# Row work of the experts in the attention turns: two units at every second turn of a head in place of one at each

## The reference, cut to what matters

```python
def peer(h):                                  # 1024 tokens, 8 heads, 16 experts of each
    q = h @ w_pq                              # scores against 2 x 128 keys, top 16 of each half,
    experts, gates = top16(sums(top16(q . keys1), top16(q . keys2)))   # best 16 of the sums
    a = gelu(einsum('td,thkd->thk', h, u_experts[experts])) * softmax(gates)
    return einsum('thk,thkd->td', a, v_experts[experts])
```

## Time and profile before

| | before |
|---|---|
| median of 3 runs | 3424.23 us |
| the profiled execution, its own time | 3428.18 us |
| its span, first to last instruction | 3426.4 us |
| TensorE busy | 2763.8 us (81%) |
| VectorE busy | 2176.9 us (64%) |
| ScalarE busy | 1371.4 us (40%) |
| GpSimd busy | 1224.1 us (36%) |
| gathers of expert rows | 1024, 1073.81 MB, 76.3% of 16 engines' span |
| mean DMA rate over the span | 364 GB/s |
| DMA busy share, slices 7 to 40 of 40 | 0.9 or more in nearly all |
| attention turns of groups 1, 2, 3 | about 665 to 790, 1412 to 1556, 2194 to 2334 us |

### The profile page before, as it was taken

One profiled execution on the slowest core, in us unless ns is written; L12 is line 12 of the kernel. 1 busy time (PEld: TensorE's weight loads), 2 busy tenths in 40 slices (PEclk: granted clock), 3 DMA queues, 4 the chain that ended last, 5 costly groups with the idle time before them and its releaser, 6 DMA issues.

```text
span 3426.4 us, 29234 instructions
## 1 busy us (share of the span) xinstructions
PE 2763.8 (81%) x8208; PEld 1489.1 (43%) x8208; DVE 2176.9 (64%) x4668; ACT 1371.4 (40%) x3703; POOL 1224.1 (36%) x1051
## 2 busy tenths in 40 slices
PE   7988878788887789788888689798887866666666
PEld 7665455354334355454335355364334322222222
DVE  1121156876774778766775767766675787777766
ACT  1112123493533343573533332583533333333333
POOL 0000013443443344334443333334343444544553
PEclk9997989999998999899998899899998889889988
DMA  6322359999999999989999999989999999999998
GB/s 239 135 99 92 129 221 382 418 382 418 427 413 386 401 425 426 375 319 376 422 427 404 385 402 397 368 334 376 420 415 402 424 426 427 427 426 415 426 427 351
DMA packets 187458, 1247.42 MB, mean 364 GB/s; under 512 B 22048, under 2 KB 31264, under 8 KB 41376
## 3 DMA queue, kind: packets, MB, share of 16 engines
q0 software_dynamic: 147456, 1073.81, 76.3%
q1 hardware_dynamic: 36384, 154.98, 11.6%
q10 hardware_dynamic: 3456, 16.78, 1.2%
HBM read 1224.77 MB, written 20.71 MB: 364 GB/s over the span
## 4 chain that ended last, share of the span: by engine, by line
PE 42%; DMA 33%; DVE 9%; ACT 6%; issue 4%; POOL 3%; DVEq 2%; ACTq 1%; POOLq 0%; SPq 0%
DMA rows<-in_experts,idx 28%; PE ps L906 17%; PE ps L939 10%; PE ps L925 6%; POOL rows L608 3%; DMA wbuf<-in_w_conv 3%; DVE rows L1291 2%; DVE acc_v L1302 2%; PE ps L957 2%; PE ps L890 1%; ACT L767 1%; DMA wbuf<-in_w_pq 1%; PE ps L1091 1%; PE ps L970 1%; PE ps L975 1%
## 5 line engine op out<-in xcount | busy, mean ns | idle before, releaser
L608 POOL DMA_INDIRECT rows<-in_experts,idx x1024 | 1220.4, 1192 | 2178.0 <-PE ps L906 1175.8
L906 PE MATMUL ps<-rows,diag 128*128 128x512 f32 x3072 | 1584.8, 656 | 355.5 <-ACT diag L664 321.4
L1291 DVE CUSTOM_DVE_ANT_0 rows<-rows,hn 128x1024 f32<-128x1024 f32 x1024 | 1236.7, 1223 | 682.0 <-DMA rows<-in_experts,idx 666.0
L906 PEld LDWEIGHTS ps<-rows,diag 128*128 128x128 f32 x3072 | 616.2, 209 | 1165.1 <-issue 591.2
L653 ACT ACTIVATE gelu<-dots 128x1 f32<-128x1 f32 x1024 | 206.6, 202 | 1383.8 <-DVE dots L1291 1369.9
L939 PE MATMUL ps<-T,wbuf 128*128 128x256 f32 x1600 | 399.7, 403 | 95.0 <-DMA wbuf<-in_w_conv 47.8
L939 PEld LDWEIGHTS ps<-T,wbuf 128*128 128x128 f32 x1600 | 320.2, 202 | 197.0 <-DMA wbuf<-in_w_conv 53.5
L925 PE MATMUL ps<-wbuf,T 128*128 128x512 f32 x768 | 362.1, 610 | 18.8 <-ACT T L815 7.5
L664 ACT ACTIVATE diag<-ident,weight 128x128 f32<-128x128 f32 x768 | 308.5, 402 | 75.3 <-PE ps L906 11.9
L657 ACT ACTIVATE weight<-gelu,gate 128x1 f32<-128x1 f32 x1024 | 301.7, 295 | 74.8 <-DVE gate L1270 2.9
L1302 DVE SCALAR_TENSOR_TENSOR acc_v<-rows,weight,acc_v 128x1024 f32<-128x1024 f32 x256 | 327.7, 1280 | 1.6 <-ACT weight L657 1.6
(11 more groups left out here) (200 smaller groups left out, 1824.3 us busy)
## 6 DMA issues: line engine op xcount, KB each, us to landing
wbuf<-in_w_conv SPq DMA_DIRECT2D x24, 1024.0 KB, 10.0
wbuf<-in_w_o SPq DMA_DIRECT2D x16, 1024.0 KB, 9.0
wbuf<-cross_a SPq DMA_DIRECT2D x16, 1024.0 KB, 9.3
wbuf<-cross_b SPq DMA_DIRECT2D x16, 1024.0 KB, 9.1
wbuf<-in_w_pq SPq DMA_DIRECT2D x16, 1024.0 KB, 9.4
rows<-in_experts,idx POOLq DMA_INDIRECT x1024, 12.3
wbuf<-in_w_cq SPq DMA_DIRECT2D x8, 768.0 KB, 8.5
wbuf<-in_w_ckvr SPq DMA_DIRECT2D x8, 576.0 KB, 6.8
```

The lines of the kernel that those rows point to most:

```text
L608: pool.indirect_dma_start(out=rows[n % RR][:], out_offset=None, in_=w["experts"][:, :], in_offset=bass.IndirectOffsetOnAxis(ap=idx[:, b % ...
L906: mm = pe.matmul(ps[:, 6 + half, :], diag[:, m % DIAGS, :], rows[n % RR][:, D + half * HALFC:D + (half + 1) * HALFC], start=(k == 0), stop ...
L1291: dve.tensor_tensor_reduce(out=rows[n % RR][:, 0:D], in0=rows[n % RR][:, 0:D], in1=hn[:, b % 3, :], scale=1.0, scalar=0.0, op0=ALU.mult, o ...
```

## The change

In the three loops over turns of a head, an engine takes two units at every even turn, and none at the odd ones. There are 20 turns, so 10 times 2 units where there were 20 times 1. Nothing else is changed.

```diff
 (ScalarE)
                 for i in range(HH + 5):
-                    if i < HH + 4:
-                        take(work, ROOM["head"])
+                    if i < HH + 4 and i % 2 == 0:
+                        take(work, 2 * ROOM["head"])
 (TensorE)
                     if 3 <= i < HH + 3:
                         turn_probs(i - 3, 0)
-                    take(work, ROOM["head"])
+                    if i % 2 == 0:
+                        take(work, 2 * ROOM["head"])
                     if i >= 4:
                         weigh(i - 4)
 (VectorE)
                 for i in range(HH + 4):
-                    take(work, ROOM["head"])
+                    if i % 2 == 0:
+                        take(work, 2 * ROOM["head"])
                     if i < HH:
                         biggest(i)
```

## The result

The changed kernel takes 3442.36 us (median of 8 runs), the kernel before 3421.1 us in its 8 runs: a ratio of 1.0056, with a 95% interval of 1.0034 to 1.0078. It is slower, by about 19 us by the ratio and by 21 us between the medians, just outside the 17 us within which the prediction saw no change that can be told. A second comparison gave 1.0059 [1.0042, 1.0077]. The profiled execution took 3448.18 us with a span of 3446.3, 19.9 us more than before.

What follows compares the result with a forecast made beforehand. Transfers were taken to bound the kernel nearly everywhere; 7.3 - 2 - 3 + 12.3 - 2 gave +12.6 us, so 3437 us (+0.37%), no change that can be told, leaning slower, with a range of 3418 to 3456.

Steps and rivals of the forecast that it cites:

- The bound: Whole kernel: transfers bound it nearly everywhere; attention group 1 close to that limit, group 2 not, group 3 nearly TensorE-bound.
- What it saves: ScalarE in the attention stages: about 14 table loads fewer per group, 18 us each, 54 us over three groups.
- The ring: Attention rounds: VectorE's units, ScalarE's tail, exp, score, maximum wait in a loop; 12.04, 13.75, 14.0 us; chance 0.72.
- piece: VectorE, within the ring: one piece of the choice of experts per round, taken at 1.8 us, ends 1.0 and 2.3.
- the copy's 0.95: Six rounds of each group: one copy of outputs, 0.95 us, added to the sum of the rounds.
- entry: Start of each attention stage: item 3's score waits behind one more unit, 4.1 us, in three groups +12.3 us.
- exit: Behind item 15: one unit fewer is left; group 1 gives back 0 to 4.7 us, taken at -2, elsewhere nothing.
- the clock rival: TensorE in groups 1 and 3: longer waits halve its clock as in group 2; +30 us, 3454; chance 0.12.
- The sum: Three attention stages: rounds +7.3, -2, -3, entry +12.3, exit -2, in all +12.6 us.
- The ends of the range: The forecast's own range: -6 us below and about +28 above, so 3418 to 3452.
- The table loads': Rival, attention stages: table loads were the limit and the ring isn't; -38 us, 3386; chance 0.10.
- nothing moves: Rival, attention stages: transfers, TensorE and an equal ring in group 2 still set the pace; 3424; chance 0.06.

Runs made afterwards that it cites:

- without table loads: The kernel before with Copy in place of gelu, so no table load stands in the turns: ratio 0.9909 [0.9878, 0.9940].
- second profile: The changed kernel run once more with nothing altered, for a second profile: ratio 1.0059 [1.0042, 1.0077] against the kernel before.
- second pair: Changed kernel and kernel before, each run once more unaltered and profiled again: ratios 1.0059 and 0.9971 against the kernel before.
- 8 buffers: The changed kernel with 8 buffers for the diagonal matrices in place of 4: ratio 1.0040 [1.0014, 1.0066] against the kernel before.
- the ring broken: The changed kernel with VectorE taking its two units one turn earlier than ScalarE and TensorE: 3403.48 us, ratio 0.9939 against the kernel before.

## Why the prediction was right, and where its sizes were off

**The bound.** That group 2 and not group 1 had room, group 3 being near TensorE's limit, held: without table loads the stages fell by 5.4, 28.6 and 7.3 us.

**What it saves.** 14 loads a group were counted, 40 went in all, 13.3 a group.

**The ring.** Its terms stand in the trace one by one. In the round shown the piece took 2.3 us to the next product where 1.8 was taken as the mean, and the score's way to its maximum 1.39 us where 1.29 was: 12.04 + 0.5 + 0.1 is the 12.66 measured. The sum can be made for each round of group 1, with that round's own piece in place of 1.8 and the copy's 0.95 in the fifth:

| round of group 1 | piece | sum | measured | TensorE at half clock |
|---|---|---|---|---|
| 1 | 1.0 | 11.2 | 11.4 | 0 |
| 2 | 2.3 | 12.5 | 12.7 | 0 |
| 3 | 2.0 | 12.2 | 12.3 | 0 |
| 4 | 1.1 | 11.4 | 12.8 | 6.8 |
| 5 | 2.3 | 13.5 | 13.7 | 0 |
| 6 | 1.7 | 12.0 | 12.8 | 6.8 |

Every round at full clock is met within 0.2 us, and the two with a half-clock stretch are 1.4 and 0.8 over. In the second profile the stretches lie in rounds 3 and 5, and these are the ones that are 0.5 and 0.6 over; the others are 0.1 to 0.3 over. So most of the 0.4 us by which the mean round (12.6) lies above the sum with its copy (12.2) is the clock, and little is the ring.

**The stages were right in part by luck.** What each part was to change, and what it changed in the two pairs of profiles (us; rounds, entry to item 3's score, exit behind item 15's):

| | summed | first pair | second pair |
|---|---|---|---|
| group 1 | +7.3, +4.1, -2 | +9.7, +1.5, -1.6 | +6.4, +2.5, -0.5 |
| group 2 | -2, +4.1, 0 | +0.7, +5.9, -2.6 | -4.1, +5.4, -4.7 |
| group 3 | -3, +4.1, 0 | +2.0, +3.2, +3.8 | +2.1, +3.1, +3.8 |

Group 1's stage was to be +9.4 and was +9.6, then +8.4, but in the first pair its rounds were 2.4 us over and its entry 2.6 under. The exit of group 2 gave back 2.6 and 4.7 us where nothing was taken. The kernel before is no fixed mark either: its six rounds of group 1 took 65.9 and 68.2 us.

**Group 3 is the term of the sum that was mis-sized.** It was taken at -3 for the rounds, +4.1 for the entry and 0 for the exit, +1.1 in all, and came to +8.9 and +9.0. Five of its rounds took 14.3 us against 14.0. The rest lies where TensorE was at half clock: one round of 17.9 us, and 3.8 us more in the exit, where the prediction had nothing since VectorE isn't last there. So the clock rival was partly right: in group 3 above all, and by about 2 us in the rounds of group 1. Group 3's stage with 8 buffers, where the half-clock stretches are fewer, is 7.9 us shorter. By the clock records inside its group 3 stage the changed kernel was at the lower level for 31.5 us (31.6 in its second profile), the kernel before for 14.6 (14.8), the one with 8 buffers for 11.8. Why it stayed low so much longer with 4 buffers than with 8 was not settled. The sign given for this rival, a clock under about 0.9 in group 1, could not decide: it was 0.88 there before the change and 0.87 after.

**The entry.** From the last copy of keys to item 3's score the stages took 26.9, 26.4 and 28.1 us and take 28.4, 32.3 and 31.2: +10.5 where +12.3 was summed, and +11.0 in the second pair. The total is near, but the forecast had it as 4.1 us in each group, and it was 1.5, 5.9 and 3.1.

**The sum.** +12.6 was forecast, +19 measured by the ratio. In the profiles the three stages gained 22.6 us, 10 more than summed: 7.8 of them in group 3, 2.0 in group 2 and 0.2 in group 1. The rest of the kernel took 2.7 us less, so the span gained 19.9. The ends of the range don't follow from their terms: the low end's add up to -3.4 us, not -6 (7.3 - 7 - 3 + 4 - 4.7), and the high end's to +27. The measured time lies inside either way.

**The rivals.** The table loads' was right in what it said of the kernel before and wrong in that no other ring would take over. That nothing moves doesn't fit: two comparisons gave 1.0056 and 1.0059, twice the 0.3% by which an identical program differed from itself, and groups 1 and 3 were longer in both pairs of profiles. Of the signs named in advance VectorE's wait ahead of the odd maximum, the DMA share of 0.92 (0.95 in the second profile) and the table loads (20 in group 1's stage) came as named. Rounds did not quite: 12.6, 15.0 and 14.9 us on the mean against 12.0, 13.8 and 14.0, and the sums were made for full clock. Item 3's score was to be 4 us later in each group; it was 3.5 later on the mean of the three, with 1.5 to 5.9 in the single ones. ScalarE's busy time fell by 48 us, 6 less than 54.

## What to carry to other kernels

Before calls are grouped by function table, see whether the bunched calls come to stand in a chain that some other engine's program order closes; here that turned the saving into a loss. Follow, for each value that the bunch produces, who waits for it, and what stands behind that in the producer's own program. Here the saving needed one more line, the producer's work moved one turn ahead of its consumer; with it the version takes 3403 us, 0.6% less than the kernel before and 1.2% less than the change alone. Before a count of busy time is believed, look at which engine waits for which in one steady round: the sum of that ring, with each round's own work in it, gave group 1's rounds at full clock to 0.3 us.

## What the runs showed that was not expected

The two-turn rounds of group 2 were 13.5 to 16.7 us in the kernel before, with stretches at half clock in all its profiles; with the ring broken and no load in the odd turns they were 11.9 us in five rounds of six, and 12.4 with the copy of outputs in it; the clock of that stage was 0.95, and its half-clock stretches all lay ahead of these rounds. That the shorter waits are why it held its clock was not tested; a part of the gain, from 13.5 us at full clock to the 14.9 it really took, is in no sum made for full clock. TensorE's bursts of 12 row matmuls took 5.32 us at full clock and 7.51 where part of them ran at half.
